# Moving two small constants ahead of the weight ring in SBUF

## What is computed

```
h = rms_norm(x, g)
x = x + (silu(h @ w_gate) * (h @ w_up)) @ w_down
...
hid = silu(einsum('becd,edf->becf', xe, w_gate)) * einsum('becd,edf->becf', xe, w_up)
ye  = einsum('becf,efd->becd', hid, w_down) * gate
```

## Time and profile before

| | |
|---|---|
| median of 3 runs | 1721.89 us (1718.8 to 1723.64) |
| profiled execution, its own time | 1728.77 us |
| span from its first to its last instruction | 1727.0 us |
| mean granted TensorE clock | 0.949 of full speed |
| TensorE matmul busy | 1515.3 us, 88% |
| VectorE, ScalarE, GpSimd busy | 51%, 39%, 9% |
| DMA | 417.13 MB, mean 242 GB/s |

### The profile page before, as it was taken

The page is one execution under the profiler, slowest core; times in us unless marked ns, Lnnn a source line. Parts: engine busy times, 40 slices in busy tenths (PEclk is TensorE's granted clock), DMA queues, the critical chain, the costliest instruction groups (busy, mean ns, idle before and its releaser), DMA issues.

```text
span 1727.0 us, 34156 instructions
## 1 busy us (share of the span) xinstructions
PE 1515.3 (88%) x14322; PEld 1318.9 (76%) x14322; DVE 875.6 (51%) x1233; ACT 665.7 (39%) x898; POOL 148.3 (9%) x189
## 2 busy tenths in 40 slices
PE   9999999999998999999999999899998555565556
PEld 8999999988998999998898899688974332333333
DVE  5776466645676756665576689866641000000001
ACT  5444454435435445543555845435442000000001
POOL 5900000000000000000106002040010000000000
PEclk9999999999999999999999999899999788877878
DMA  7665656774743766666454254002899999999996
GB/s 253 228 221 187 199 160 180 217 268 154 262 149 122 268 214 165 188 180 216 138 164 148 82 164 147 26 27 76 314 396 418 432 428 434 427 432 431 430 430 286
DMA packets 238194, 417.13 MB, mean 242 GB/s; under 512 B 13731, under 2 KB 213994, under 8 KB 228074
## 3 DMA queue, kind: packets, MB, share of 16 engines
q1 hardware_dynamic: 237881, 414.62, 66.4%
q10 hardware_dynamic: 176, 0.53, 0.1%
HBM read 414.07 MB, written 1.06 MB: 240 GB/s over the span
## 4 chain that ended last, share of the span: by engine, by line
PE 61%; issue 28%; DVE 5%; ACT 4%; DMA 2%; POOL 1%; SPq 0%; DVEq 0%; ACTq 0%; POOLq 0%
PE bank_sums L440 9%; PE bank_sums L441 9%; PE bank_sums L442 9%; PE bank_sums L456 3%; PE bank_sums L458 3%; PE bank_sums L457 3%; PE bank_sums L1147 2%; PE bank_sums L1148 2%; PE bank_sums L1149 2%; ACT w_hi L243 1%; PE bank L1994 1%; PE bank_sums L468 1%; PE bank_sums L470 1%; PE bank_sums L469 1%; PE bank_sums L1994 1%
## 5 line engine op out<-in xcount | busy, mean ns | idle before, releaser
L250 DVE TENSOR_TENSOR w_lo<-w_raw,w_hi 128x2048 fp32r<-128x2048 f32 (+2 forms) x178 | 402.1, 2262 | 227.2 <-ACT w_hi L243 226.9
L243 ACT ACTIVATE w_hi<-w_raw 128x2048 fp32r<-128x2048 f32 (+2 forms) x178 | 333.6, 1879 | 150.0 <-DMA w_raw<-in_ffn_w_down_dram 47.8
L440 PE MATMUL bank_sums<-h_hi,w_hi 128*128 128x256 f32 x1152 | 324.6, 282 | 6.0 <-DVE h_lo L650 3.7
L442 PE MATMUL bank_sums<-h_hi,w_lo 128*128 128x256 f32 x1152 | 323.7, 281 | 0.0
L441 PE MATMUL bank_sums<-h_lo,w_hi 128*128 128x256 f32 x1152 | 323.6, 281 | 0.0
L2876 PE MATMUL bank<-w_exp_four,xeT 128*32 128x256 f32 x1600 | 139.3, 520 | 116.4 <-DMA w_exp_four<-in_w_gate_dram 63.5
L440 PEld LDWEIGHTS bank_sums<-h_hi,w_hi 128*128 128x128 f32 x1152 | 217.6, 189 | 7.3 <-issue 7.3
L442 PEld LDWEIGHTS bank_sums<-h_hi,w_lo 128*128 128x128 f32 x1152 | 220.5, 191 | 0.0
L441 PEld LDWEIGHTS bank_sums<-h_lo,w_hi 128*128 128x128 f32 x1152 | 217.1, 188 | 0.0
L2876 PEld LDWEIGHTS bank<-w_exp_four,xeT 128*32 128x32 f32 x1600 | 68.8, 147 | 184.9 <-issue 115.7
L3039 DVE TENSOR_TENSOR hx<-sg,bank 128x256 f32<-128x256 f32 x16 | 6.7, 422 | 282.4 <-ACT sg L3009 282.4
(11 more groups left out here) (587 smaller groups left out, 3081.6 us busy)
## 6 DMA issues: line engine op xcount, KB each, us to landing
w_exp_four<-in_w_up_dram SPq DMA_DIRECT2D x13, 4096.0 KB, 33.3
w_exp_four<-in_w_down_dram SPq DMA_DIRECT2D x13, 4096.0 KB, 33.6
w_exp_four<-in_w_gate_dram SPq DMA_DIRECT2D x12, 4096.0 KB, 34.9
w_raw<-in_ffn_w_gu_dram SPq DMA_DIRECT2D x88, 512.0 KB, 5.1
w_raw<-in_w_in_dram SPq DMA_DIRECT2D x54, 512.0 KB, 4.8
w_mod<-in_w_mod_dram SPq DMA_DIRECT2D x24, 1024.0 KB, 8.4
w_raw<-in_ffn_w_down_dram SPq DMA_DIRECT2D x44, 512.0 KB, 4.4
w_raw<-in_mem_w_kv_dram SPq DMA_DIRECT2D x32, 512.0 KB, 4.6
```

The lines of the kernel that those rows point to most:

```text
L243: e.activation(whi[slot][:, 0:w], raw[slot][:, 0:w], ACT.Copy).then_inc(S["hi_ready"], 1)
L250: e.tensor_tensor(wlo[slot][:, 0:w], raw[slot][:, 0:w], whi[slot][:, 0:w].bitcast(F32), ALU.subtract).then_inc(S["lo_ready"], 1)
L440: e.matmul(dst, whi[slot][:, lo:hi_], bh[:, k, :], start=begin, stop=False)
L442: ins = e.matmul(dst, wlo[slot][:, lo:hi_], bh[:, k, :], start=False, stop=end)
```

## The change

neg_half and eps, 32 bytes each, are placed ahead of w_raw instead of behind small. No instruction is added, taken out or moved. w_raw, w_hi, w_lo, w_mod, ident, ones, vcol and small, and what is placed by their addresses (w_exp and w_exp_four in the ring, the buffers counted from w_mod0), lie 64 bytes higher; swap1 and everything behind it lie where they lay. The weights now begin at 192 modulo 256 and the features at 64: 128 apart.

```
@@ -125,6 +125,8 @@
+    neg_half = place("neg_half", [P, 4], F32)
+    eps = place("eps", [P, 4], F32)
     raw = [place(f"w_raw{s}", [P, CHUNK_W], F32) for s in range(RING)]
     whi = [place(f"w_hi{s}", [P, CHUNK_W], F32R) for s in range(RING)]
     wlo = [place(f"w_lo{s}", [P, CHUNK_W], F32R, offset=sbuf_at[f"w_raw{s}"]) for s in range(RING)]
@@ -133,8 +135,6 @@
     small = place("small", [P, 192], F32)
-    neg_half = place("neg_half", [P, 4], F32)
-    eps = place("eps", [P, 4], F32)
     swap1 = place("swap1", [ROT, ROT], F32)
```

## The result

The changed kernel takes 1738.87 us (median of 4 runs, 1736.26 to 1740.37) against 1722.77 us (4 runs, 1718.8 to 1724.04): a ratio of 1.0086, 95% interval 1.0062 to 1.0109 (the two medians alone would give 1.0093). It is slower by 16.1 us. The forecast was 1710 us, faster.

A forecast was written before the change was run, and what follows sets the result against it. TensorE's matmul pace was taken to bound the kernel up to a weight-streaming expert stage. Half of the slow stretches turning quick gives 12 us, all else 0: 1721.9 - 12 = 1710 us, range 1694 to 1738.

The forecast's parts named there:

- TensorE sets the pace up to the experts, and what it loses reaches the end: Ahead of the weight-streaming expert stage: whatever TensorE saves brings that stage's start, and the end, forward by as much.
- 9.7 us a place: Expert stage: one of the four load places comes every 9.7 us, and this must stay so after the change.
- Two paces at one clock, with the distance as a cause: Ring matmuls of 256 columns: 113.4 or 117.7 ns at granted clock 1.00, depending on how the operands' addresses meet.
- The row of distance 0: L1365, both operands from a_hi, 0 bytes apart: 32 matmuls at 120.0 ns, taken as upper bound of the pace at 128.
- 128 lies between these two. So I take the same two paces: Ring matmuls at 128: between 64 and 192, so 113.4 and 117.7 ns again, how often each is caught left open.
- The sum: Whole kernel: half of 25 - 1.5 us gained in ring matmuls, 12 us, with 0 for constants and expert loads.
- the slow fifths: Some four fifths of about 7,300 ring matmuls, 5,840, run at 117.7 ns; all turning quick would save 25 us.
- The slower rival: Ring matmuls no longer hold the quick pace: 1728 if they fall to 117.7 ns, 1746 at 120.0; chance 0.23 including loads.
- No gain or loss from loads: Expert stage: three of four places move from 128 to 192 modulo 256; taken as 0, bounds 2 us either way.
- the two stretches of 21 us: Where the DMA share is 1.01: a transfer a tenth longer would cost up to 4 us; chance 0.04 for slower loads.
- A stretch's pace as a property of the kernel: Ring matmuls: each stretch holds one pace unbroken; quick stretches, 102 of 535 us in the profiled execution, served as the base.
- the quick fifth: Stretches at 19, 110, 421, 447, 587 and 856 us, at 113.4 ns; falling to 117.7 would cost 6 us.

## Why the prediction was wrong

- *TensorE sets the pace up to the experts, and what it loses reaches the end*: right. 10.8 of 11.3 us were lost by the gather, and 9.7 us a place stayed.
- *Two paces at one clock, with the distance as a cause*: right, and shown by the two kernels that keep the distance and move the addresses, or the reverse. The row of distance 0 was a sound witness: 120.0 ns forecast, 120.1 measured.
- *"128 lies between these two. So I take the same two paces"*: this is the step that failed. 64 and 192 are mirror images, and their likeness shows that swapping roles changes little at that distance; it says nothing of what lies between. At 128 the pace is 118.7 ns in both roles, with a few stretches at 120.0, and never 113.4 or 117.7. At 32 and 96 there is none of 113.4 either. Why 128 is worse than 64 stays open: the runs show the paces by distance and no mechanism behind them.
- *The sum*: the forecast took half of the slow fifths to be quick, -12 us. The measured term is +1.9 ns x 7,300 = +13.9 us, and +1.8 us for the 512-column products, of which the forecast said at most -1.
- *The slower rival* had the mechanism, the quick pace is no longer held, with 6 us if all fell to 117.7 and 24 us at 120.0. It came out between, at 16.1, at a pace of its own that neither price had. It was given 0.19 (the 0.23 of slower less 0.04 for loads), and the range ended at 1738, below the 1738.87 measured.
- *No gain or loss from loads*: right, 431 and 432 GB/s with three of the places 64 bytes further. Of the two stretches of 21 us that the forecast put at a DMA share of 1.01, the second, from 627 us, stood at 0.98; nothing hung on it.
- *A stretch's pace as a property of the kernel*: the forecast read the quick fifth from one execution and added and subtracted by it. Three executions gave three sets, with 23%, 37% and 26% of the rounds quick, so a fifth was one draw and 1727.0 the longest of three spans.

The Trainium skill, "SBUF — State Buffer", section "Who interferes with whom", has it that TensorE never waits on anyone, and that its two read ports, one for the moving operand and one for the weight load, are independent. Whether another engine makes it wait for SBUF no run here tests. Within TensorE its operands' addresses alone moved the pace from 113.3 to 120.9 ns, which independent reads would not explain; whether the time is lost in the reads is not shown.

## What to carry to other kernels

Where float32r matmuls of 256 columns follow each other with a weight load each, the starts of the two operands modulo 256 bytes are worth a sweep: they moved this kernel by 1.5%, from 1716 to 1742 us, at no cost. Measure every distance rather than interpolate, in both roles and at each number of columns: distance 0 was the worst common distance for 256 columns and the best for 512. Look at several stretches and more than one execution, since one stretch can show one of two or three paces. Read the pace from starts over a long stretch; durations differ by 2.5% only, 276 to 283 ns.

## What was not expected

- One program, two paces: at distance 64 a stretch of 1,000 matmuls holds 113.4 or 117.7 ns without a break, and which one differs between executions, and between two feed-forwards of the same code. At 96 a stretch holds one of 117.3, 118.7 and 120.0, and at 128 one of 118.7 and 120.0.
- The order of distances is not that of size: 120.1 ns at 0, 118.4 at 32, 113.3 or 117.8 at 64, 120.0 or 118.7 at 96, 118.7 at 128 (weights stationary, both feed-forwards), and with the features stationary 116.7 at 32.
- For 512 columns the order is another one: 226.8 ns at 0, 229.0 or 233.3 at 64, 232.4 at 128, 233.3 at 32 and 192, 233.4 at 96.
- w_hi 64 and w_lo 192 above the features hold 113.3 ns where one common distance only catches it; exchanged, they do not, and with h_lo moved by 128 as well it is 120.9. No rule that covers these was found. Distances that are no multiple of 32 were not measured.
